# Two FFNs that host a depthwise convolution: work put in the stages in front, three down slabs of each split

## The reference, cut to what matters

```python
def dwconv(x, w, b):
    k = w.shape[0]
    pad = (k - 1) // 2
    y = lax.conv_general_dilated(x, w[:, None, :], window_strides=(1,), padding=[(pad, pad)],
                                 dimension_numbers=('NWC', 'WIO', 'NWC'),
                                 feature_group_count=x.shape[-1])
    return y + b

def conformer_conv(h, w_pw1, b_pw1, w_dw, b_dw, ln_g, ln_b, w_pw2, b_pw2):
    u = h @ w_pw1 + b_pw1
    a, g = jnp.split(u, 2, axis=-1)
    v = a * jax.nn.sigmoid(g)
    v = dwconv(v, w_dw, b_dw)
    v = jax.nn.silu(layernorm(v, ln_g, ln_b))
    return v @ w_pw2 + b_pw2

def conv_ffn(h, w_up, w_dw, b_dw, w_down):
    u = dwconv(h @ w_up, w_dw, b_dw)
    a, b = jnp.split(u, 2, axis=-1)
    return (jax.nn.silu(a) * b) @ w_down
```

## Time and profile before

| | us |
|---|---|
| median of 3 runs | 1395.15 |
| lowest, highest | 1395.05, 1398.12 |
| the profiled execution | 1393.4 |
| its span in the trace | 1391.6 |
| PE busy | 1368.5 (98%) |
| DVE busy | 963.3 (69%) |
| ACT busy | 824.7 (59%) |
| POOL busy | 461.4 (33%) |

### The profile page before, as it was taken

The page is one execution under the profiler, slowest core; times in us unless marked ns, Lnnn a source line. Parts: engine busy times, 40 slices in busy tenths (PEclk is TensorE's granted clock), DMA queues, the critical chain, the costliest instruction groups (busy, mean ns, idle before and its releaser), DMA issues.

```text
span 1391.6 us, 27113 instructions
## 1 busy us (share of the span) xinstructions
PE 1368.5 (98%) x10606; PEld 1270.7 (91%) x10606; DVE 963.3 (69%) x1298; ACT 824.7 (59%) x1190; POOL 461.4 (33%) x190
## 2 busy tenths in 40 slices
PE   7999999999999999999999999999999999999997
PEld 4788889999999999899999999999998968999996
DVE  3322674857899987779899979766667696654446
ACT  3632564646788837567888565555544486644554
POOL 2452444244232221232222201655552201233332
PEclk9999999999999999999999999999999999999999
DMA  8775774455344434774444447555554613455551
GB/s 323 256 294 212 267 277 182 166 211 182 122 182 181 177 151 186 263 280 158 163 157 162 181 190 254 226 212 211 211 186 186 269 45 130 182 182 181 181 185 57
DMA packets 39573, 272.04 MB, mean 195 GB/s; under 512 B 4612, under 2 KB 5892, under 8 KB 6974
## 3 DMA queue, kind: packets, MB, share of 16 engines
q1 hardware_dynamic: 39486, 270.81, 52.2%
HBM read 269.73 MB, written 1.06 MB: 195 GB/s over the span
## 4 chain that ended last, share of the span: by engine, by line
PE 91%; DVE 4%; ACT 2%; DMA 2%; issue 1%; SPq 0%; DVEq 0%; ACTq 0%
PE ps L1985 23%; PE ps L1986 23%; PE ps L1987 23%; PE ps L655 10%; PE ps L2131 3%; PE ps L2022 2%; DMA raw<-w_dram 2%; PE ps L2032 1%; PE ps L2499 1%; PE ps L2485 1%; DVE wlo L1340 1%; ACT whi L845 1%; PE ps L2434 1%; PE ps L2181 1%; DVE tiny L1833 0%
## 5 line engine op out<-in xcount | busy, mean ns | idle before, releaser
L803 POOL TENSOR_TENSOR wlo<-raw,whi 128x1024 fp32r<-128x1024 f32 (+2 forms) x181 | 459.2, 2538 | 909.9 <-ACT whi L845 909.9
L845 ACT ACTIVATE whi<-raw 128x2048 fp32r<-128x2048 f32 x181 | 345.5, 1911 | 391.2 <-PE ps L1987 229.3
L1340 DVE TENSOR_TENSOR wlo<-raw,whi 128x1024 fp32r<-128x1024 f32 (+2 forms) x181 | 312.7, 1729 | 319.0 <-ACT whi L845 318.0
L1985 PE MATMUL ps<-h_hi,whi 128*128 128x256 f32 x1232 | 354.1, 287 | 0.6 <-ACT gates L1002 0.6
L1986 PE MATMUL ps<-h_lo,whi 128*128 128x256 f32 x1232 | 348.4, 283 | 0.0
L1987 PE MATMUL ps<-h_hi,wlo 128*128 128x256 f32 x1232 | 348.4, 283 | 0.0
L1985 PE MATMUL ps<-g_hi,whi 128*128 128x256 f32 x1040 | 298.4, 287 | 0.0
L1986 PE MATMUL ps<-g_lo,whi 128*128 128x256 f32 x1040 | 294.2, 283 | 0.0
L1987 PE MATMUL ps<-g_hi,wlo 128*128 128x256 f32 x1040 | 294.1, 283 | 0.0
L1985 PEld LDWEIGHTS ps<-h_hi,whi 128*128 128x128 f32 x1232 | 236.0, 192 | 8.7 <-issue 6.3
L1986 PEld LDWEIGHTS ps<-h_lo,whi 128*128 128x128 f32 x1232 | 236.1, 192 | 0.8
(11 more groups left out here) (317 smaller groups left out, 1858.0 us busy)
## 6 DMA issues: line engine op xcount, KB each, us to landing
raw<-w_dram SPq DMA_DIRECT2D x243, 1024.0 KB, 4.9
sra<-w_dram SPq DMA_DIRECT2D x2, 1024.0 KB, 5.9
mqk<-w_dram SPq DMA_DIRECT2D x2, 1024.0 KB, 6.4
brev<-w_dram SPq DMA_DIRECT2D x2, 1024.0 KB, 7.3
gates<-w_dram SPq DMA_DIRECT2D x2, 1024.0 KB, 8.5
xlat<-xT_dram SPq DMA_DIRECT2D x2, 512.0 KB, 4.6
brev<-w_first_keys_dram SPq DMA_DIRECT2D x1, 1024.0 KB, 9.3
brev<-bias_rows SPq DMA_DIRECT2D x1, 1024.0 KB, 8.4
```

The lines of the kernel that those rows point to most:

```text
L803: pool.tensor_tensor(wlo[:, g.slot, part], raw[:, g.slot, part], whi[:, g.slot, part].bitcast(F32), ALU.subtract).then_inc(lo2_done, 1)
L845: act.activation(whi[:, g.slot, :], raw[:, g.slot, :], ACT.Copy).then_inc(hi_done, 1)
L1340: dve.tensor_tensor(wlo[:, g.slot, part], raw[:, g.slot, part], whi[:, g.slot, part].bitcast(F32), ALU.subtract)\
L1985: pe.matmul(out, w[0], x[0], start=start, stop=False, skip_group_check=True)
```

## The change

In both hosts:

- The first tap is written in pieces during the stages in front, as soon as a piece of `vpad` is there, and so is one own tap, k = 2 (`early_tap`). ACT makes products 0 and 1 there as well; for ffn0 their last two tiles come at the first place of iteration 0.
- Down slabs 2, 4 and 6 are split, with `m_hi` and `m_lo` for those iterations and semaphores of their own (`hostmid_hi`, `hostmid_lo`).
- There are 25 products in place of 22 and, beside the first tap, five own taps in place of eight: the early one and those of iterations 1, 3, 5 and 7. Iterations 0 to 7 add three products each. Iterations 0, 2, 4 and 6 have no own tap.
- ACT's and DVE's loops over the hosts' iterations 2 to 7 are written out.

```diff
-PRODUCTS = 22
+DOWN_SPLIT = (2, 4, 6)
+ADD_SLOTS = [(j, at) for j in range(NJ - 3) for at in range(3)] + [(NJ - 3, 0)]
+OWN_SLOTS = [j for j in range(1, NJ - 3) if j not in DOWN_SPLIT]
+PRODUCTS = len(ADD_SLOTS)
+OWN_TAPS = [2] + [4 * j for j in OWN_SLOTS]
+PRODUCT_TAPS = [k for k in range(1, CONV_TAPS) if k not in OWN_TAPS]
...
-            out.append(use != ffn or (i >= 4 and i % 3 == 1))
+            out.append(use != ffn or (i >= 4 and i % 3 == 1 and (i - 4) // 3 not in DOWN_SPLIT))
```

In `up` of `ffn_act`:

```diff
+                if whole and j - 2 in DOWN_SPLIT:
+                    act.wait_ge(hostmid_lo, host_mid(f, j - 2))
                 tap(1, j, par)
```

In `split` of `ffn_act`:

```diff
-                if whole:
+                if whole and not host_split(j, par):
                     return
                 act.wait_ge(mid_f, j + (f * NJ + 1))
+                if whole:
+                    act.wait_ge(slab_done, down_slab(b0, j - 2) + 1)
+                    act.activation(m_hi[:, par, :, :], cvb[:, par, :, :], ACT.Copy).then_inc(hostmid_hi, 2)
+                    return
...
             if host:
-                with act.Fori(0, 3) as jj:
-                    for u in range(2):
-                        up(Slab(b0 + 5 + 3 * u, 2, jj), 2 * jj + (2 + u), u, False)
-                for j in (NJ - 3, NJ - 2):
-                    up(Slab(b0 + 3 * j - 1), j, j % 2, False)
+                for j in range(2, NJ - 1):
+                    g = Slab(b0 + 3 * j - 1)
+                    up(g, j, j % 2, False)
+                    hi(g + (2 + RING))
+                    split(j, j % 2, False)
```

In `pair` of `ffn_dve`:

```diff
                 if down:
                     lo(g + (2 + RING))
+                if whole and host_split(j, par):
+                    dve.wait_ge(hostmid_hi, host_mid(f, j))
+                    dve.tensor_tensor(m_lo[:, par, :, :], cvb[:, par, :, :], m_hi[:, par, :, :].bitcast(F32), ALU.subtract)\
+                       .then_inc(hostmid_lo, 2)
```

In `down` of `ffn_pe`:

```diff
-                    pe.wait_ge(mid_lo, j + (fs * NJ + 1))
+                    if whole:
+                        pe.wait_ge(hostmid_lo, host_mid(f, j))
+                    else:
+                        pe.wait_ge(mid_lo, j + (fs * NJ + 1))
```

In the stage in front of ffn0, ACT:

```diff
                 hi(Slab(b1 + 4 + RING))
+                act.wait_ge(xlo_done, KT // 2 * n + KT // 2)
+                product(q, 0, 0, 6)
                 hi(Slab(b1 + 5 + RING))
                 glu(q, 3, b1 + 5)
+                product(q, 1, 0, 6)
```

In the same stage, DVE:

```diff
                 glu(q, 2)
+                dwconv_first(q, 4, 6)
                 lo(Slab(b1 + 4 + RING))
+                early_tap(2, 6)
                 lo(Slab(b1 + 5 + RING))
                 glu(q, 3)
+                dwconv_first(q, 6, KT)
+                early_tap(6, KT)
```

In `host` of `conv_dve`:

```diff
+                    if (j, at) in ADD_SLOTS:
+                        n = ADD_SLOTS.index((j, at))
+                        add_product(q, n, bufs[n % 2])
+                        if at == 1 and j in OWN_SLOTS:
+                            dve.wait_ge(prod_used, n + 1 + PRODUCTS * q)
+                            own_tap(OWN_TAPS[1 + OWN_SLOTS.index(j)])
```

More of the change, by code:

```diff
@@ L597, in ffn_dve @@
             pair(Slab(b0 + 2), 1, 1, True, hosted(1, 1))
-            with dve.Fori(0, 3 if host else 4) as jj:
-                order.enter(jj, 8 + (2 * KT if host else 0))
-                for u in range(2):
-                    j = 2 * jj + (2 + u)
-                    pair(Slab(b0 + 5 + 3 * u, 2, jj), j, u, True, hosted(j, u))
-                order.leave(3 if host else 4)
             if host:
-                for j in (NJ - 3, NJ - 2):
+                for j in range(2, NJ - 1):
                     pair(Slab(b0 + 3 * j - 1), j, j % 2, True, hosted(j, j % 2))
+            else:
+                with dve.Fori(0, 4) as jj:
+                    order.enter(jj, 8)
+                    for u in range(2):
+                        pair(Slab(b0 + 5 + 3 * u, 2, jj), 2 * jj + (2 + u), u, True, None)
+                    order.leave(4)
             g = Slab(b0 + 3 * NJ - 4)
@@ L632, in down @@
             def down(g, j, par, first=False, last=False):
-                if whole:
+                plain = whole and not host_split(j, par)
+                if plain:
                     pe.wait_ge(landed[g.slot], g.landings())
@@ L934, in ln_silu, with product @@
                     upper(KT - 2)
-            def product(q, n, k, buf):
-                if not isinstance(n, int) or n >= 2:
+            def product(q, n, t0=0, t1=KT):
+                k, buf = PRODUCT_TAPS[n], (bufA, bufB)[n % 2]
+                if n >= 2:
                     act.wait_ge(prod_used, n + (PRODUCTS * q - 1))
-                for t in range(KT):
-                    w = cols[:, bass.ds(KT * k + (COL["dw_w"][0] + t), 1)]
-                    ins = act.activation(buf[:, t * T:t * T + T], vpad[:, t, bass.ds(k, T)], ACT.Copy, scale=w)
-                ins.then_inc(prod_done, 1)
+                else:
+                    act.wait_ge(v_done, 4 * q + t1 // 2)
+                    act.wait_ge(pads_done, 2)
+                for t in range(t0, t1):
+                    ins = act.activation(buf[:, t * T:t * T + T], vpad[:, t, k:k + T], ACT.Copy, scale=col("dw_w", KT * k + t))
+                if t1 == KT:
+                    ins.then_inc(prod_done, 1)
@@ L957, in host @@
-                    if isinstance(j, int) and (j, at) == (NJ - 2, 1):
+                    if (j, at) == (0, 0) and q == 0:
+                        product(q, 0, 6, KT)
+                        product(q, 1, 6, KT)
+                    if (j, at) in ADD_SLOTS[1:-1]:
+                        product(q, ADD_SLOTS.index((j, at)) + 1)
+                    if (j, at) == (NJ - 2, 1):
                         ln_squares(q)
-                    if isinstance(j, int) and (j, at) == (NJ - 1, 0):
+                    if (j, at) == (NJ - 1, 0):
@@ L960, in host @@
                         ln_root(q)
[L961 removed]
+                    if (j, at) == (NJ - 1, 1):
                         ln_silu(q, out, 0, KT // 2)
[L963 removed]
+                    if (j, at) == (NJ - 1, 2):
                         ln_silu(q, out, KT // 2, KT)
@@ L1161, in _ @@
             c = hi_to(c, "pw1_lat", 7)
+            product(1, 0, 0, 6)
             c = hi_to(c, "ffn_ctx", 0)
@@ L1166, in _ @@
             c = hi_to(c, "ffn_ctx", 2)
+            product(1, 0, 6, KT)
+            product(1, 1)
             c = ffn_act(act, hi, 1, "ffn_ctx", squares_after(1, xctx, 12), conv_act(1, g_hi), ahead=2)
@@ L1458, in add_product @@
                 dve.wait_ge(dve_order, order.value())
-                if not isinstance(n, int) or n:
+                if n:
                     dve.wait_ge(prod_used, n + PRODUCTS * q)
@@ L1462, in add_product, with own_tap, early_tap @@
                 dve.tensor_tensor(flat(acc[:, :, :]), flat(acc[:, :, :]), buf[:, :], ALU.add).then_inc(prod_used, 1)
-            def own_tap(q, n, k):
-                dve.wait_ge(prod_used, n + PRODUCTS * q)
-                for t in range(KT):
-                    w = cols[:, bass.ds(KT * k + (COL["dw_w"][0] + t), 1)]
-                    order.mark(dve.scalar_tensor_tensor(acc[:, t, :], vpad[:, t, bass.ds(k, T)], w, acc[:, t, :], ALU.mult, ALU.add))
+            def own_tap(k, t0=0, t1=KT):
+                for t in range(t0, t1):
+                    order.mark(dve.scalar_tensor_tensor(acc[:, t, :], vpad[:, t, k:k + T], col("dw_w", KT * k + t), acc[:, t, :],
+                                                        ALU.mult, ALU.add))
+            def early_tap(t0, t1):
+                dve.wait_ge(dve_order, order.value())
+                own_tap(OWN_TAPS[0], t0, t1)
             def conv_dve(q, out):
```

50 lines of the change are left out of this document (21 added, 29 removed).

## The result

| | before | after |
|---|---|---|
| median | 1395.1 (4 runs) | 1416.27 (4 runs) |
| lowest, highest | 1394.98, 1398.12 | 1415.55, 1417.02 |
| profiled execution, its span | 1393.4, 1391.6 | 1415.55, 1412.0 |
| mean granted clock of PE | 0.997 | 0.992 |

The ratio is 1.0143, with a 95% interval of 1.0126 to 1.016. The change costs 21 us. The forecast was 1405 with a range of 1391 to 1416: the direction was right, the size was not, and the time lies just above the range.

The account below looks back on a forecast made before the run. PE bounded the old kernel; after the change a DVE-ACT-DVE chain between split slabs would. +2.2 us without collisions and 7.5 for collisions gave +9.7 on 1393.4; with 1.75 to the median, 1405, range 1391 to 1416.

Parts of the forecast that it names:

- What is saved: PE in the hosts: a split down slab takes 5.75 us instead of 6.91, 1.16 saved, 7.0 for six.
- The chain of a pair, 37.2 us: Hosts, DVE and ACT, from one split slab's upper half to the next one's: 37.2 us, where PE asks 35.66.
- The first split slab's m_lo at 399.1: First host, iteration 2: DVE ends m_lo at 399.1, PE wants it at 397.67 and stalls 1.5 us.
- Sum without collisions, +2.2 us: Both hosts: 1.5 + 2 × (37.2 − 36.82) − 1.16 = +1.1 us each, +2.2 in all.
- Collisions, 3.5 in each host: DVE subtractions started when POOL is already at the slab: 3.5 a host at 1.07 us, 7.5 for both.
- the sentence that DVE is late at all four: Hosts, new order: DVE comes late at all four up-slab subtractions of a pair of iterations.
- Case (d): Hosts: every late DVE subtraction collides with POOL, +23.6 us, 1419; with some missing, from 1410 on; chance 0.13.
- The single stop of 1.5 us: PE at the first split slab of a host: it stalls 1.5 us waiting for m_lo.
- The pieces in front, the longer loops, the stages behind, 0: Stages in front: pieces go into gaps waiting for PE; loops written out; DVE catches up before layer norm; nothing charged.
- The sentence that DVE has no third add past the last split slab: Hosts past the last split slab: DVE has no third add and catches up before the layer norm needs it.
- Case (a), as meant: Hosts: the chain is shorter than added up, PE stays the bound, 7.0 us saved: 1388.2, partly 1391; chance 0.15.

Follow-up runs that it names:

- Both edits: Changed kernel with ACT's upper half of the split slab right after silu and POOL starting after DVE's part in the hosts: 1392.09 us, ratio 0.9969.
- POOL behind DVE: Changed kernel with POOL in the hosts starting each slab only when DVE is through with its part: 1399.52 us, ratio 1.0026.
- the kernel with the upper half first: Changed kernel with ACT making the split down slab's upper half right after silu, ahead of the iteration's last product: 1398.22 us, ratio 1.0014.
- the last run: Changed kernel, ACT's upper half right after silu, POOL starting after DVE's part only from each host's fourth slab on: 1392.26 us, ratio 0.9968.

## Why the prediction was off, point by point

- **What is saved**, 1.16 us for each split slab, and PE's 35.66 us for a pair: right. Both edits come to 35.96.
- **The chain of a pair, 37.2 us**: right, 36.96 in the run with POOL behind DVE, which keeps the order and has the same one overlap. Its two waits are where the prediction put them (ACT 2.47 for the add, DVE 2.37 for the upper half), and m_lo takes 1.76 for 1.8.
- **The first split slab's m_lo at 399.1**: it ended at 399.82. The 0.7 are one collision in the run-up (a subtraction at 384.50 with 2.83), less small gains. I had put half a one there, in the term of the collisions.
- **Sum without collisions, +2.2 us**: right. POOL behind DVE gives +0.8 and +2.7, and 1.5 of the second are the stretch between the hosts: 2.0 are left. That is in part luck. The stop at the first split slab was 1.45 us where 1.5 was forecast, but it ended with POOL's late part and not with m_lo.
- **Collisions, 3.5 in each host: this is the step that failed.** There were seven on the way in the first host (three in each pair, one in the run-up) and eight in the second (the two of its run-up at 640.00 and 680.24). So the term was 15 × 1.07 = 16.1 us and not 7.5. The price of one, 1.07, was right, the mechanism too, and so was the sentence that DVE is late at all four. But I scaled the number down from the old loop, where it was one of two, and where DVE had slack. In the new order DVE never catches up, so the pattern of one pair repeats exactly: three of four, each time the same three. Case (d), every one, with some missing, was the nearer one; the old frequency was no evidence for an order in which DVE starts late each time.
- **PE's clock was not in the sum at all,** and cost some 1.8 us here. It is a second term that failed, put at nothing without a reason. With both, the forecast's +9.7 becomes 9.7 + 8.6 + 1.8 = 20.1, where the ruler has 19.9. In the kernel after, PE stands 4.3 us ahead of the second split slab of the first host and 2.8 ahead of the last one of the second. The windows behind both:

```profile
440.10:446.00 5.90, 5.79 (x27) 5.82 (x28) 5.87 (x6) 5.63 (x11) 2.20 (x2) 0.50 0.88 290
776.05:781.90 5.85, 5.81 (x36) 5.81 (x37) 5.81 (x6) 5.66 (x11) 2.16 (x2) 0.71 0.79 270
```

  Within the hosts this is mostly hidden, since the next m_lo comes from DVE's chain. Behind the last split slab PE sets the pace again and pays: from 776.05 to slab 7 at 795.11 are 19.06 us where 17.25 are asked, 1.8 us; in the first host 17.64 (480.28 to 497.92), 0.4 us, there with the granted clock at 1.00, so those 0.4 are not the clock's. The single stop of 1.5 us that I forecast would most likely have cost nothing more: behind the stops of 1.02 to 1.50 us in these traces the clock stayed at 1.00.
- **Balance.** First host: 0.8 + 7 × 1.07 + 0.4 = 8.7, measured 8.4. Second: 1.2 + 8 × 1.07 + 1.8 = 11.6, measured 11.5. The first terms come from the run with POOL behind DVE and hold its own waits for POOL, so an agreement within 0.3 us is closer than the sum deserves.
- **The pieces in front, the longer loops, the stages behind, 0**: right as long as PE sets the pace, by the run without a split slab. With split slabs they are not priced apart. In the second host of the kernel after, the chain that ended last leaves PE at 631.4, in the stage in front, and runs over pieces of products on ACT (633.99 to 638.09) and the collided subtraction at 640.00 up to slab 2. The sentence that DVE has no third add past the last split slab misreads the kernel: iteration 7 still adds three products. It cost nothing, since slab 8 follows slab 7 after 18.84 us before and after.
- **Case (a), as meant**, was out of reach for the reason given against it, and came true in the main once that reason and the collisions were both taken away: PE is the bound, and 4.7 of the 7.0 us are there.

## What to carry to other kernels

When work is taken off the engine that sets the pace, sum the other engines as a chain from one of the repeated points to the next, with the waits in it, and not as busy time: here the sum of work was 34.7 us and the chain 37.2, while PE asked 35.7 (36.8 before). If the chain becomes the longer one, take every collision on it at its full price and near its worst rate (three of four here), because an engine that is always late can meet the same neighbour in the same place in every round, and allow for a stretch at the lower clock behind PE's longer stops. Before splitting more work, look at the order inside the chain: issuing the one operation that another engine waits for ahead of one that itself waits, and starting GpSimd behind VectorE where they share a slab, turned 1.4% slower into 0.3% faster.

## What the runs showed of the hardware that I had not expected

- **Short stops of PE can lower its clock.** Behind stops of 2.5 and 4.0 us the granted clock was 0.73 and 0.63 in the next 6 us, and 0.50 in 440.10 to 446.00, which is 1.2 GHz throughout; the others mix 1.2 and 2.4. The price, in the kernel with one split slab, was 1.7 and 2.3 us on top of the stops. The length of the stop doesn't decide it alone. Behind the first stop of the kernel after, 2.51 us as in the run with one split slab, the clock stayed up, and so it did behind one of two nearly equal stops (1.87 and 1.86 us) of the kernel with the upper half first. The windows behind these three:

```profile
399.97:405.97 6.00, 6.00 (x50) 6.00 (x51) 5.96 (x6) 5.52 (x11) 2.31 (x2) 1.00 0.82 298
726.55:732.55 6.00, 6.00 (x50) 6.00 (x51) 5.96 (x6) 6.00 (x12) 1.68 (x2) 1.00 0.86 289
764.37:770.37 6.00, 6.00 (x37) 6.00 (x38) 5.96 (x6) 6.00 (x12) 1.68 (x2) 0.72 0.79 274
```

  What else decides is open. The Trainium skill (TensorE: Matmul & The Clock Gate, "What's actually happening") names the same two levels.
- **Who pays in a collision of DVE and POOL is not simply who starts later.** POOL began at 424.46 and DVE at 424.72, and DVE took 2.85; POOL began at 418.37, DVE at 419.15, and DVE took its 1.75 while POOL took 3.68. The rule that the prediction quoted from the Trainium skill (SBUF — State Buffer, "Who interferes with whom"), that the first to issue holds the port for its whole instruction, fits the former pair of rows and not the latter. In each of these pairs DVE's add was still running when POOL's row began, so both were waiting to start when it ended, and one of the two had the whole delay. What decides it was not tried.
- **M_lo of 512 columns takes 0.68 us alone and 1.76 beside POOL**, so the price of an overlap goes by POOL's own time (1.3 us for 512 columns once nothing overlaps) and not by a share of the delayed instruction: 1.07 on an instruction of 1.75 and 1.08 on one of 0.68. When m_lo began 0.71 us after POOL, it lost only 0.45 (434.96 in the last run).
